# Two transformer blocks on one core: raw tokens turned before their norm, the norm's factor at the projections' reads, and three reorderings

## The chip, the cores and the metric

One NeuronCore of one Trainium2 chip runs the whole program. The time is device microseconds of one execution; three runs of the kernel before took 998.76, 1000.24 and 1002.35 us, median 1000.24. Lower is better.

## What is computed

256 tokens of width 1024, float32, go through two blocks. Cut to what matters here:

```python
def first_block(x, ...):                       # x: (1, 256, 1024)
    h = rms_norm(x, norm_mix)                  # x / sqrt(mean(x^2) + 1e-6) * gain, per token
    q_a, k_a, v_a, q_b, k_b, v_b, g_a, g_b = split(h @ w_in)
    q_a, k_a, q_b, k_b = their own rms_norm per head of 64
    o_a = neighbourhood_attention(q_a, k_a, v_a, rpb)   # 8 heads, a bias gathered from rpb
    o_b = sliding_window_attention(q_b, k_b, v_b, sink, t5_table)
    y = sigmoid(g_a) * (o_a @ w_branch_a) + sigmoid(g_b) * (o_b @ w_branch_b)
    x = x + y @ w_out
    h = rms_norm(x, norm_ffn)
    return x + (silu(h @ w_gate) * (h @ w_up)) @ w_down

def second_block(x, ...):                      # retention + RWKV, then 32 experts of width 512, top 2
    x = x + mixers(rms_norm(x)) @ w_out_2
    x = x + hier_moe(rms_norm(x), ...)         # reads all 32 experts' weights, 192 MB
    return rms_norm(x) * gain
```

rms_norm divides each token by one number, so `rms_norm(x) @ W` equals that number times `(x * gain) @ W`, row by row.

## The kernel before

The program is written out by hand, one instruction list per engine, joined by semaphores. There is no scheduler: each engine's order is the order of the code in its block. A matrix product in float32 precision is made of three passes over rounded parts. Weights and features are each split into a high part (ScalarE copies them rounded, `high_part(g)`, L2183, for weight chunk g; `high_features` and `high_resid` for features) and a low part (VectorE subtracts the high part, `low_part(g)`, L2642; `low` and `resid_low` for features), and TensorE multiplies high by high, high by low and low by high (L1195 to L1197, and L1330 with L1332 in the feed-forward part).

**The front.** SyncE loads the tokens `x` in two halves of 128, then the weights of `w_in`. TensorE first runs 19 idle products (`idle`, L1160). ScalarE squares and sums each half of x (`squares(0)`, L2162) and takes the root (L2163), VectorE inverts it and scales the tokens into `xn` (`norm()`, L2612), TensorE turns `xn` (`norm_T`, L1168), VectorE multiplies by the gain while it reads the turned tokens from PSUM (`moved`, L2651; this waits for `cols`, where the gains lie), ScalarE makes their high parts (L2211), VectorE their low parts (L2657). `moved` and the copies work on quarters (half h of the features, half t of the tokens). `norm_T` also puts the tokens in another order (columns of the 4 x 64 grid in blocks of 8), so that the projected rows come out in that order. Then TensorE runs the projections p1,0 to p1,8 of `w_in`; p1,0 is `first_unit` (L1274), whose first weights ScalarE splits in two steps (`first_high`, L2190). ScalarE copies each projected bank out of PSUM (L2272, L2270 and L2320, plain copies).

**The bias of the first attention.** GpSimd copies `rpb` to DRAM in four DMAs (L1055), waits for weight slot 2 and for the four, and gathers the bias from there with 32 DMAs (L1065) into `biasA_raw`; after them come its copies of the values (`vspan`, `vb`), then 16 loads of the second bias. VectorE adds the window's mask (`biasA_raw` to `biasA`, 8 instructions, L2760). In the code this stands after the heads' norms of p1,0 and p1,1 (`low_part(8)`) and ahead of the sums of squares of p1,3 (L2730, L2734) and of `low_part(9)`, on which the projection p1,5,0 waits. p1,4's sums, the first softmax step `softmax_in(0)` (L2712 to L2721), the norms of q_b and k_b (L2749, L2747) and `low_part(10)` follow.

**The attention loop.** Step i of 9 has on TensorE scores(i), the turning of the probabilities of step i-1 (`turned`), half a projection unit, and the weighted sum of step i-1 (`weighted`, L1471 and L1142). On VectorE it has `softmax_in(i)`, `low_part`, and `weighted(i-1)`, which begins with the copy of the turned probabilities out of PSUM (L2767), on which TensorE's weighted sum waits.

**The residual's turns.** While the output projection `wo` runs, the new x is turned again for the feed-forward part in four pieces j = 0 to 3 of 256 features (`resid_turned`, L1540, and `resid_T` for the last, L1150), each after VectorE has added the piece's projection to x (L2833). VectorE applies the gain (`resid_gain`, L2625), ScalarE makes the high part (`high_resid`, L2196) and VectorE the low part (`resid_low`, L2634). Piece 3 is turned before the first product of the gate; the gate's product takes its features in the order k = 0 to 5 and then 6 to 7. `squares(1)` on ScalarE and `diagonals(1)` on VectorE then make the token factors that `spread_tiles(1)` (L1191) needs inside the first `up` product.

**The experts.** In the last half of the span SyncE streams the experts' weights; each load waits until the place that it fills has been read.

Of the kernel before, what the change touches and what calls it, by code (L numbers as in the profile page):

```python
# [342 lines left out]
def build(nc, A, out):  # L343
# [13 lines left out]
    with ExitStack() as ctx:  # L357
# [73 lines left out]
        bonus = st[:, 160:176]  # L431
        minus_k_a = st[:, 180:184]
# [156 lines left out]
        xn_ready = sem("xn_ready")  # L589
        diag_ready = sem("diag_ready")  # L590
# [73 lines left out]
        rpb_copies = nc.dram_tensor("rpb_copies", (ROWS_A * RUN + 2, 8, ROWS_A * 31), F32, kind="Internal").ap()  # L664
        vb_rows = nc.dram_tensor("vb_rows", (T, P), F32, kind="Internal").ap()
# [245 lines left out]
        def _(sp):  # L911
# [45 lines left out]
            def moe_stream(r, first):  # L957
                if first:
# [40 lines left out]
                    sp.wait_ge(xn_ready, 2 * NT)  # L999
# [51 lines left out]
        def _(pool):  # L1051
# [5 lines left out]
            pool.wait_ge(slot_in[2], 16)  # L1057
# [64 lines left out]
        def _(pe):  # L1122
# [144 lines left out]
            def first_unit(name):  # L1267
# [50 lines left out]
            def features_both(key, name, c, lows=None, between=None):  # L1318
# [74 lines left out]
            idle(19)  # L1393
            pe.wait_ge(ident_in, 16)
            norm_T()

# [155 lines left out]
            resid_T(1, 3, ("wo", 1, 1))  # L1552
# [582 lines left out]
            pe.wait_ge(xn_ready, 2 * NT)  # L2135
# [13 lines left out]
        def _(act):  # L2149
# [88 lines left out]
            high_part(2)  # L2238
# [17 lines left out]
            for n in range(9):  # L2256
# [12 lines left out]
                if u == 4:  # L2269
                    empty(fn(nat[:, :, 2048:2304], bank("p1", 4, 0).rearrange("p (t n) -> p t n", t=NT), ACT.Copy), "p1", 4, 0)  # L2270
                else:
                    empty(fn(nat[:, c, 512 * u:512 * u + 512], bank("p1", u, c), ACT.Copy), "p1", u, c)  # L2272
# [1069 lines left out]
```

## Time and profile before

| | |
|---|---|
| median of three runs | 1000.24 us (998.76 to 1002.35) |
| the profiled execution, its own time | 998.47 us |
| its span | 996.7 us |
| TensorE busy | 867.2 us (87%) |
| VectorE busy | 443.7 us (45%) |
| ScalarE busy | 328.1 us (33%) |
| GpSimd busy | 48.2 us (5%) |
| DMA moved | 293.44 MB, mean 294 GB/s |
| TensorE's granted clock | full in the first 23 of the page's 40 slices, 0.7 to 0.9 and over in the rest |

Busy shares are means over parts with different limits. A TensorE instruction's length in the timeline includes its filling and draining; the distance between two starts is what it costs in a row (0.23 us for 512 columns, 0.12 us for 256).

### The profile page before, as it was taken

What the parts mean: (1) busy time and instruction counts of PE and PEld (TensorE: products, weight loads), DVE (VectorE), ACT (ScalarE), POOL (GpSimd) and SP (SyncE); (2) the same over time, 40 slices, a digit from 0 to 9 for tenths busy, and PEclk for the clock granted to TensorE, in tenths of its full rate; (3) what the DMA queues carried; (4) which work ended last, traced back from release to release, by engine and by line L of the source; (5) the groups of instructions that cost most, each with busy time, mean ns of one, the idle gap of its engine ahead of it and who ended that gap; (6) DMA issues with size and microseconds to landing.
All of it is one profiled execution on the core that took longest, in us unless ns stands there. A gap on an engine that the chain in (4) does not pass through costs nothing.

```text
span 996.7 us, 16047 instructions
## 1 busy us (share of the span) xinstructions
PE 867.2 (87%) x6902; PEld 596.3 (60%) x6902; DVE 443.7 (45%) x593; ACT 328.1 (33%) x433; POOL 48.2 (5%) x80
## 2 busy tenths in 40 slices
PE   9999999899999999999989987667768676785785
PEld 8889888888888889989989532221312221131223
DVE  6766777688776348898865310000100000010002
ACT  6466663665465328645523300000000000000002
POOL 1825000000000000000100000000000000000000
PEclk9999999999999999999999999878978877788889
DMA  9998335486555455452369999999999999999995
GB/s 321 219 339 196 110 114 180 132 283 207 181 171 207 172 177 203 147 192 86 117 203 410 369 429 418 430 428 427 428 429 429 427 428 429 427 430 428 423 424 205
DMA packets 76762, 293.44 MB, mean 294 GB/s; under 512 B 6550, under 2 KB 33430, under 8 KB 63385
## 3 DMA queue, kind: packets, MB, share of 16 engines
q1 hardware_dynamic: 70496, 283.91, 73.4%
q0 software_dynamic: 2592, 3.20, 2.0%
q10 hardware_dynamic: 3608, 5.39, 1.6%
q8 instruction: 49, 0.80, 0.3%
q14 instruction: 17, 0.13, 0.0%
HBM read 288.65 MB, written 3.41 MB: 293 GB/s over the span
## 4 chain that ended last, share of the span: by engine, by line
PE 58%; DMA 31%; DVE 5%; POOL 2%; issue 2%; SPq 1%; ACT 1%; DVEq 0%; ACTq 0%; POOLq 0%
DMA arena<-in_w_up 11%; DMA arena<-in_w_gate 9%; PE psum L1330 8%; DMA arena<-in_w_down 8%; PE psum L2056 7%; PE psum L1195 5%; PE psum L1197 5%; PE psum L1196 5%; PE psum L1357 4%; PE psum L1332 4%; PE psum L2084 3%; PE psum L1731 2%; POOL arena L1065 2%; DVE ring_rounded L2642 1%; DMA arena<-in_w_in 1%
## 5 line engine op out<-in xcount | busy, mean ns | idle before, releaser
L2056 PE MATMUL psum<-arena,featL 128*32 128x512 f32 x1008 | 161.6, 701 | 57.4 <-DMA arena<-in_w_up 38.9
L2642 DVE TENSOR_TENSOR ring_rounded<-arena,hi_rounded 128x2048 fp32r<-128x2048 f32 x75 | 171.6, 2290 | 59.7 <-ACT hi_rounded L2183 58.5
L2183 ACT ACTIVATE hi_rounded<-arena 128x2048 fp32r<-128x2048 f32 x76 | 144.8, 1912 | 85.7 <-DMA arena<-in_w_up 19.8
L2056 PEld LDWEIGHTS psum<-arena,featL 128*32 128x32 f32 x1008 | 37.7, 125 | 168.2 <-issue 85.9
L1330 PE MATMUL psum<-ffn_in_rounded,hi_rounded 128*128 128x512 f32 x352 | 122.3, 394 | 0.0
L2084 PE MATMUL psum<-arena,featT 128*32 128x512 f32 x424 | 76.7, 729 | 38.1 <-DMA arena<-in_w_down 33.8
L1195 PE MATMUL psum<-hi_rounded,featT_rounded 128*128 128x256 f32 (+1 forms) x320 | 101.2, 316 | 1.1 <-DVE ring_rounded L2642 0.9
L1197 PE MATMUL psum<-hi_rounded,featL_rounded 128*128 128x256 f32 (+1 forms) x320 | 99.2, 310 | 0.0
L1196 PE MATMUL psum<-ring_rounded,featT_rounded 128*128 128x256 f32 (+1 forms) x320 | 99.1, 310 | 0.0
L1332 PE MATMUL psum<-ffn_in_rounded,ring_rounded 128*128 128x256 f32 x352 | 97.8, 278 | 0.0
L1330 PEld LDWEIGHTS psum<-ffn_in_rounded,hi_rounded 128*128 128x128 f32 x352 | 66.1, 188 | 15.2
L3228 DVE TENSOR_TENSOR featT<-featT,psum 128x512 f32<-128x512 f32 x8 | 8.2, 1031 | 149.1 <-PE psum L2056 149.1
L2084 PEld LDWEIGHTS psum<-arena,featT 128*32 128x32 f32 x424 | 16.9, 130 | 88.8 <-DMA arena<-in_w_down 46.9
L1332 PEld LDWEIGHTS psum<-ffn_in_rounded,ring_rounded 128*128 128x128 f32 x352 | 66.2, 188 | 0.0
L1195 PEld LDWEIGHTS psum<-hi_rounded,featT_rounded 128*128 128x128 f32 x320 | 61.0, 191 | 4.8 <-ACT arena L2270 1.1
L1197 PEld LDWEIGHTS psum<-hi_rounded,featL_rounded 128*128 128x128 f32 x320 | 61.0, 191 | 3.2
L1196 PEld LDWEIGHTS psum<-ring_rounded,featT_rounded 128*128 128x128 f32 x320 | 61.1, 191 | 3.0
L3213 DVE TENSOR_TENSOR featL<-psum,gain 128x256 f32<-128x256 f32 x32 | 13.6, 425 | 105.3 <-PE psum L2036 105.3
L2545 ACT ACTIVATE featT<-psum 128x512 f32<-128x512 f32 x8 | 4.8, 597 | 163.0 <-PE psum L2056 163.0
L3241 DVE COPY featL<-psum 128x512 f32<-128x512 f32 x7 | 4.8, 692 | 119.2 <-PE psum L2084 119.2
L2547 ACT ACTIVATE featT<-psum 128x512 f32<-128x512 f32 x8 | 4.8, 597 | 132.5 <-PE psum L2072 132.5
L2036 PEld LDWEIGHTS psum<-featT,xn 128*128 128x128 f32 x256 | 32.5, 204 | 17.1 <-issue 14.4
(389 smaller groups left out, 1289.2 us busy)
## 6 DMA issues: line engine op xcount, KB each, us to landing
arena<-in_w_down SPq DMA_DIRECT2D x32, 2048.0 KB, 17.9
arena<-in_w_gate SPq DMA_DIRECT2D x28, 2048.0 KB, 20.7
arena<-in_w_up SPq DMA_DIRECT2D x24, 2048.0 KB, 23.8
arena<-in_w_in SPq DMA_DIRECT2D x14, 2048.0 KB, 9.6
arena<-in_w_up SPq DMA_DIRECT2D x25, 1024.0 KB, 9.1
arena<-in_w_gate SPq DMA_DIRECT2D x14, 1024.0 KB, 5.5
arena<-in_w_down SPq DMA_DIRECT2D x7, 1024.0 KB, 9.8
arena<-in_w_out SPq DMA_DIRECT2D x3, 2048.0 KB, 7.7
```

What stands on the lines that cost most here:

```text
L1065: nc.gpsimd.dma_start(biasA_raw[at % P + RUN * r:at % P + RUN * r + RUN, at // P].rearrange("p h (r c) -> p (h r) c", c=SPAN), src).then_i ...
L1195: mm(o, lhs[0], rhs[0], start=start, stop=False, skip_group_check=True)
L1196: mm(o, lhs[0], rhs[1], start=False, stop=False, skip_group_check=True)
L1197: return mm(o, lhs[1], rhs[0], start=False, stop=stop, skip_group_check=True)
L1330: mm(banks[f].rearrange("p (s t) -> p s t", s=2), hi_cols(g, k, P * f, P), ffn_both[:, :, k, :], start=k == 0, stop=k == DK - 1, skip_grou ...
L1332: ins = mm(banks[f][:, 0:T], lo_cols(g, k, P * f, P), ffn_parts[0][:, k, :], start=False, stop=k == DK - 1, skip_group_check=True)
L1357: return mm(b[:, f, :], w(g, k, P * f, P), r[:, k, :], start=(f, k) == (0, 0) and w is hi_cols and r is featR, stop=stop, skip_group_check ...
L2036: ins = mm(b[:, k - ks[0], :], xn[:, t, k * P:(k + 1) * P], G[:, t].rearrange("p e s -> p (e s)"), start=t == 0, stop=t == NT - 1)
L2056: ins = mm(psum[32 * j:32 * j + 32, MB[4 + m], :], xg[:, 4 * half + k, 32 * j:32 * j + 32], weights(m, half, j, 512 * k), start=half == 0 ...
L2084: return mm(psum[32 * j:32 * j + 32, MB[4 + half], :], hhT[:, k, 32 * j:32 * j + 32], weights(2, k // 2, j, at_), start=k == 0, stop=k == ...
L2183: fn(high, view, ACT.Copy).then_inc(hi_ready, 1)
L2642: tt(low, view, high.bitcast(F32), ALU.subtract).then_inc(lo_ready, 1)
```

## The change

The tokens are turned as they land; the norm's factor is made later and applied as the scale of ScalarE's copies out of PSUM. Since the projected rows stand in the grid's order, GpSimd takes the factors through DRAM into that order (`token_rms`). The number of idle products goes from 19 ahead of the turns to 10 ahead and 6 behind. Four orders change with it: the quarters and first weights at the start, the mask on the bias, the copy of the probabilities, and the residual's turns.

```diff
 @@ GpSimd
-            pool.wait_ge(slot_in[2], 16)
+            pool.wait_ge(rms0_ready, NT)
+            by_place = rms_rows.rearrange("(b r c) a -> r b (c a)", r=ROWS_A, c=RUN)
+            for r in range(ROWS_A):
+                at = GRID_W * (r % 2)
+                nc.gpsimd.dma_start(by_place[r], st[at:at + GRID_W, r // 2:r // 2 + 1], allow_slow_non_contiguous=True)\
+                    .then_inc(rms0_stored, 16)
+            pool.wait_ge(rms0_stored, 16 * ROWS_A)
+            nc.gpsimd.dma_start(token_rms, rms_rows.rearrange("(t p) a -> p (t a)", p=P), allow_slow_non_contiguous=True)\
+                .then_inc(rms0_in, 16)
             pool.wait_ge(rpb_copied, 16 * ROWS_A)
 @@ TensorE
-                        pe.wait_ge(xn_ready, t + 1)
+                        pe.wait_ge(x_in[t], 16)
-                            ins = tr(b[:, k], xn[:, t, (4 * h + k) * P:(4 * h + k + 1) * P], ident)
+                            ins = tr(b[:, k], x[:, t, (4 * h + k) * P:(4 * h + k + 1) * P], ident)
...
+                pe.wait_ge(feat_lo, NT)
+                for t in range(NT):
+                    part(0, t, featLR, hi_cols, range(2))
                 pe.wait_ge(hi_ready, chunk_of[name, 0] + 1)
                 for t in range(NT):
                     part(0, t, featR, hi_cols, range(2, 4))
-                pe.wait_ge(feat_lo, NT)
-                for t in range(NT):
-                    part(0, t, featLR, hi_cols)
+                    part(0, t, featLR, hi_cols, range(2, 4))
...
-                for ks in (range(DK),) if lows is None else (range(0, 6), range(6, DK)):
+                for ks in (range(DK),) if lows is None else (range(0, 4), range(4, 6), range(6, DK)):
                     for f in range(2):
+                        if lows is not None and (ks[0], f) == (0, 1):
+                            resid_turned(turned_bank, 3, ("wo", 1, 1))
...
-            idle(19)
+            idle(10)
             pe.wait_ge(ident_in, 16)
             norm_T()
+            idle(6)
...
-            resid_T(1, 3, ("wo", 1, 1))
+            turned_bank = begin("nt", 1, 3)
 @@ ScalarE
-            squares(0, lambda t: act.wait_ge(x_in[t], 16))
+            fn(warm[:], eps_col[:, 0:1], ACT.Sqrt)
+            high_features((0, 0), (0, 1))
             first_high(0, first_hi)
-            high_features((0, 0), (0, 1))
             first_high(1, hi_ready)
+            high_features((1, 0))
             high_part(1)
-            high_features((1, 0), (1, 1))
+            high_features((1, 1))
+            squares(0, lambda t: act.wait_ge(x_in[t], 16), warmed=True)
+            high_part(2)
...
-                    empty(fn(nat[:, c, 512 * u:512 * u + 512], bank("p1", u, c), ACT.Copy), "p1", u, c)
+                    act.wait_ge(rms0_in, 16)
+                    empty(fn(nat[:, c, 512 * u:512 * u + 512], bank("p1", u, c), ACT.Copy, scale=token_rms[:, c:c + 1]), "p1", u, c)
...
-                    ins = fn(sig[:, :, 256 * i:256 * i + 256], bank("p1", u, c).rearrange("p (t n) -> p t n", t=NT), ACT.Copy)
+                    for t in range(NT):
+                        ins = fn(sig[:, t, 256 * i:256 * i + 256], bank("p1", u, c)[:, 256 * t:256 * t + 256], ACT.Copy,
+                                 scale=token_rms[:, t:t + 1])
...
-            high_resid(1, 0)
+            for j in range(2):
+                high_resid(1, j)
             high_part(first["ffn", 0])
-            high_resid(1, 1)
+            high_resid(1, 2)
             high_part(first["ffn", 0] + 1)
-            for j in range(2, 4):
-                high_resid(1, j)
+            high_resid(1, 3)
 @@ VectorE
-                for t in range(NT):
-                    ts(xn[:, t, :], x[:, t, :], inverse(0, t), None, ALU.mult).then_inc(xn_ready, 1)
...
+                for t in range(NT):
+                    dve.wait_ge(rms_ready, t + 1)
+                    s = st[:, t:t + 1]
+                    nc.vector.reciprocal(s, s).then_inc(rms0_ready, 1)
...
             for u, lo, H in units_:
                 wait_emptied(dve, "p1", u, 0 if u == 4 else 1)
                 q = nat[:, :, lo:lo + 64 * H]
+                if u == 4:
+                    mask_bias()
...
-                if i < 8:
-                    if i:
-                        softmax_in(i)
+                if 0 < i < 8:
+                    softmax_in(i)
+                if i >= 1:
+                    turned(i - 1)
+                if i < 8:
                     low_part(first["p1", 5] + i + 1)
...
-            for c in range(2):
+            projected(0)
+            low_part(first["ffn", 0])
+            resid_gain(1, 2)
+            projected(1)
+            resid_low(1, 2)
+            resid_gain(1, 3)
+            resid_low(1, 3)
             low_part(first["ffn", 0] + 1)
```

`mask_bias` holds the eight additions and their waits as before; `turned` is the copy that began `weighted`; `projected(c)` is the addition to x (L2833 before). The three `xn_ready` counts elsewhere fall by two. p1,4's copy is split in two like the gates'.

The places at which the order matters most:

VectorE around the heads' norms, before. `ring_rounded` rows are `low_part` (the one with hi_rounded_50 is chunk 8, with hi_rounded_59 chunk 9, with hi_rounded_56 chunk 10), `arena<-arena,cst` is the mask, `arena<-psum,arena` the first softmax step.

```order
L2749 TENSOR_TENSOR arena<-arena,st 128x512 x4
L2642 TENSOR_TENSOR ring_rounded<-arena,hi_rounded_50 128x2048
L2760 TENSOR_TENSOR arena<-arena,cst 128x8x32 x8
L2730 TENSOR_TENSOR arena<-arena 128x1024
L2734 TENSOR_REDUCE st<-arena 128x16
L2642 TENSOR_TENSOR ring_rounded<-arena,hi_rounded_59 128x8x256
L2730 TENSOR_TENSOR arena<-arena 128x2x128
L2734 TENSOR_REDUCE st<-arena 128x4
L2712 SCALAR_TENSOR_TENSOR arena<-psum,arena 128x2x128
```

The same place in the changed kernel:

```order
L2786 TENSOR_TENSOR arena<-arena,st 128x512 x4
L2661 TENSOR_TENSOR ring_rounded<-arena,hi_rounded_50 128x2048
L2767 TENSOR_TENSOR arena<-arena 128x1024
L2771 TENSOR_REDUCE st<-arena 128x16
L2661 TENSOR_TENSOR ring_rounded<-arena,hi_rounded_59 128x8x256
L2754 TENSOR_TENSOR arena<-arena,cst 128x8x32 x8
L2767 TENSOR_TENSOR arena<-arena 128x2x128
L2771 TENSOR_REDUCE st<-arena 128x4
L2734 SCALAR_TENSOR_TENSOR arena<-psum,arena 128x2x128
```

The eight additions moved from ahead of p1,3's sums and chunk 9 to right behind them, ahead of p1,4's sums, the first softmax step and chunk 10.

VectorE during the residual's turns, in the changed kernel (`arena<-psum,cols` is `resid_gain`, `ffn_in_rounded` is `resid_low`, `x<-x,psum` the addition to x). The rows of before at this place are, from the third on, resid_low for piece 1, the addition, `low_part`, gain 2, low 2, the addition, gain 3, low 3.

```order
L2644 TENSOR_TENSOR arena<-psum,cols 128x512 x2
L2653 TENSOR_TENSOR ffn_in_rounded<-arena,ffn_in_rounded 128x512 x2
L2864 TENSOR_TENSOR x<-x,psum 128x2x256
L2661 TENSOR_TENSOR ring_rounded<-arena,hi_rounded_60 128x2048
L2644 TENSOR_TENSOR arena<-psum,cols 128x512
L2864 TENSOR_TENSOR x<-x,psum 128x2x256
L2653 TENSOR_TENSOR ffn_in_rounded<-arena,ffn_in_rounded 128x512
L2644 TENSOR_TENSOR arena<-psum,cols 128x512
L2653 TENSOR_TENSOR ffn_in_rounded<-arena,ffn_in_rounded 128x512
L2661 TENSOR_TENSOR ring_rounded<-arena,hi_rounded_58 128x2048
```

The second addition to x now stands ahead of piece 2's low part, no longer behind it.

GpSimd's DMAs, in the changed kernel:

```order
L1060 DMA rpb_copies<-in_rpb 72x1x124
L1060 DMA rpb_copies<-in_rpb 64x1x124 x2
L1060 DMA rpb_copies<-in_rpb 72x1x124
L1066 DMA rms_rows<-st 8x8x1 x4
L1069 DMA st<-rms_rows 128x2x1
L1078 DMA arena<-rpb_copies 8x32x32 x32
L1083 DMA arena<-arena 96x512
```

The five small DMAs of the factor stand ahead of the 32 loads of the bias.

## Rows read from the trace of the kernel before

**Rows 1.** The page: how busy the DMA engines are in 40 equal slices.

```profile
DMA  9998335486555455452369999999999999999995
```

**Rows 2.** TensorE's waits over the span: who for, us in total, times, longest.

```profile
PE psum L2056 <- DMA arena<-in_w_up: 38.9, 15, 4.9
...
PE psum L1195 <- DVE ring_rounded L2642: 0.9, 1, 0.9
PE psum L1142 <- DVE arena L2767: 0.9, 3, 0.3
...
PE psum L1471 <- DVE arena L2767: 0.6, 1, 0.6
```

**Rows 3.** Timeline, start: start us, us, engine, line, what, count [idle before <- releaser].

```profile
1.16 6.88 PE L1160 MATMUL psum<-late 128*128 128x128 f32 x38 [1.16 <-DVE late L2693]
1.20 0.45 ACTq L2226 DMA_DIRECT2D cols<-in_cols  x1
...
6.04 1.06 ACT L2162 ACTIVATE xn<-x 128x1024 f32<-128x1024 f32 x1
...
7.42 1.05 ACT L2190 ACTIVATE hi_rounded<-arena 128x1024 fp32r<-128x1024 f32 x1
...
7.88 2.21 PE L1168 MATMUL psum<-cst,xn 128*128 128x128 f32 x16
...
8.62 1.42 DVE L2651 TENSOR_TENSOR featL<-psum,cols 128x512 f32<-128x512 f32 x2
9.34 1.35 ACT L2211 ACTIVATE featT_rounded<-featL 128x512 fp32r<-128x512 f32 x2 [0.87 <-DVE featL L2651]
...
10.84 2.09 PE L1274 MATMUL psum<-hi_rounded,featT_rounded 128*128 128x512 f32 x8 [0.76 <-ACT featT_rounded L2211]
```

**Rows 4.** DMA issues: transfer, count, KB each, median us from issue to landing.

```profile
cols<-in_cols ACTq DMA_DIRECT2D x1, 35.0 KB, 5.0
...
rpb_copies<-in_rpb POOLq DMA_DIRECT2D x2, 34.9 KB, 5.3
...
rt<-vb_rows POOLq DMA_DIRECT2D x4, 32.0 KB, 2.4
```

**Rows 5.** Timeline of GpSimd's DMA issues.

```profile
17.18 2.44 POOL L1055 DMA_DIRECT2D rpb_copies<-in_rpb  x4 [16.72 <-DMA arena<-in_w_in]
24.88 20.27 POOL L1065 DMA_DIRECT2D arena<-rpb_copies  x31 [5.27 <-DMA rpb_copies<-in_rpb]
52.12 0.66 POOL L1065 DMA_DIRECT2D arena<-rpb_copies  x1 [6.97 <-issue]
```

**Rows 6.** Timeline, 25 to 74 us, TensorE, VectorE and ScalarE.

```profile
25.77 0.58 ACT L2272 ACTIVATE arena<-psum 128x512 f32<-128x512 f32 x1
...
32.74 0.39 PE L1195 MATMUL psum<-hi_rounded,featT_rounded 128*128 128x512 f32 x1
...
57.10 2.77 DVE L2760 TENSOR_TENSOR arena<-arena,cst 128x256 f32<-128x256 f32 x8 [7.21 <-DMA arena<-rpb_copies]
...
59.98 1.92 ACT L2183 ACTIVATE hi_rounded<-arena 128x2048 fp32r<-128x2048 f32 x1
...
62.42 2.29 DVE L2642 TENSOR_TENSOR ring_rounded<-arena,hi_rounded 128x2048 fp32r<-128x2048 f32 x1
...
69.57 2.29 DVE L2642 TENSOR_TENSOR ring_rounded<-arena,hi_rounded 128x2048 fp32r<-128x2048 f32 x1
...
73.09 0.36 PE L1195 MATMUL psum<-hi_rounded,featT_rounded 128*128 128x256 f32 x1
```

**Rows 7.** Timeline, 180 to 194 us, TensorE and ScalarE.

```profile
180.68 0.66 PE L1540 MATMUL psum<-cst,x 128*128 128x128 f32 x4 [1.03 <-DVE x L2833]
...
185.76 0.63 PE L1150 MATMUL psum<-cst,x 128*128 128x128 f32 x4 [1.54 <-DVE x L2833]
...
187.22 0.64 ACT L2196 ACTIVATE ffn_in_rounded<-arena 128x512 fp32r<-128x512 f32 x1 [3.00 <-DVE arena L2625]
...
193.16 0.61 PE L1191 MATMUL psum<-rt,cst 128*128 128x128 f32 x4
```

More of the change, by code:

```diff
@@ L431, in build @@
         bonus = st[:, 160:176]
+        token_rms = st[:, 10:10 + NT]
         minus_k_a = st[:, 180:184]
@@ L589, in build @@
         xn_ready = sem("xn_ready")
+        rms0_ready = sem("rms0_ready")
+        rms0_stored = sem("rms0_stored")
+        rms0_in = sem("rms0_in")
         diag_ready = sem("diag_ready")
@@ L2269, in _ @@
                 if u == 4:
-                    empty(fn(nat[:, :, 2048:2304], bank("p1", 4, 0).rearrange("p (t n) -> p t n", t=NT), ACT.Copy), "p1", 4, 0)
-                else:
-                    empty(fn(nat[:, c, 512 * u:512 * u + 512], bank("p1", u, c), ACT.Copy), "p1", u, c)
+                    for t in range(NT):
+                        ins = fn(nat[:, t, 2048:2304], bank("p1", 4, 0)[:, 256 * t:256 * t + 256], ACT.Copy, scale=token_rms[:, t:t + 1])
+                    empty(ins, "p1", 4, 0)
+                else:
+                    act.wait_ge(rms0_in, 16)
+                    empty(fn(nat[:, c, 512 * u:512 * u + 512], bank("p1", u, c), ACT.Copy, scale=token_rms[:, c:c + 1]), "p1", u, c)
                 if n == 7:
@@ L2670, in norm_T @@
                 low(0, 1)
+                moved(1, 0)
                 first_low(0, first_hi, first_lo)
                 first_low(1, hi_ready, lo_ready)
-                moved(1, 0)
                 moved(1, 1)
@@ L2677, in norm_T @@
                 low_part(1)
+                for t in range(NT):
+                    dve.wait_ge(rms_ready, t + 1)
+                    s = st[:, t:t + 1]
+                    nc.vector.reciprocal(s, s).then_inc(rms0_ready, 1)
             def low_moved(*key):
@@ L2721, in softmax_in, with mask_bias @@
                     ts(m, m, -1.0, None, ALU.mult).then_inc(max_ready, 1)
+            def mask_bias():
+                dve.wait_ge(params_in, PARAMS_IN)
+                dve.wait_ge(biasA_in, 16 * 8 * ROWS_A)
+                for t in range(NT):
+                    for b in range(SPAN // RUN):
+                        raw = biasA_raw[:, t].rearrange("p h (r c) -> p h r c", r=ROWS_A)[:, :, :, RUN * b:RUN * b + RUN]
+                        made = biasA[:, t].rearrange("p h (b r c) -> p h b r c", r=ROWS_A, c=RUN)[:, :, b]
+                        window = con("wina")[:, SPAN * t + RUN * b:SPAN * t + RUN * b + RUN]
+                        ins = tt(made, raw, window.unsqueeze(1).unsqueeze(1).to_broadcast([P, 8, ROWS_A, RUN]), ALU.add)
+                ins.then_inc(biasA_ready, 1)
+                dve.wait_ge(biasA_ready, 1)
             tmp = area(L1, "probT", 4, 512)[:, 0:2, :]
@@ L2751, in _, with turned @@
                     low_part(8)
-                    dve.wait_ge(params_in, PARAMS_IN)
-                    dve.wait_ge(biasA_in, 16 * 8 * ROWS_A)
-                    for t in range(NT):
-                        for b in range(SPAN // RUN):
-                            raw = biasA_raw[:, t].rearrange("p h (r c) -> p h r c", r=ROWS_A)[:, :, :, RUN * b:RUN * b + RUN]
-                            made = biasA[:, t].rearrange("p h (b r c) -> p h b r c", r=ROWS_A, c=RUN)[:, :, b]
-                            window = con("wina")[:, SPAN * t + RUN * b:SPAN * t + RUN * b + RUN]
-                            ins = tt(made, raw, window.unsqueeze(1).unsqueeze(1).to_broadcast([P, 8, ROWS_A, RUN]), ALU.add)
-                    ins.then_inc(biasA_ready, 1)
-                    dve.wait_ge(biasA_ready, 1)
+            def turned(i):
+                wait_filled(dve, "PT", i, 1)
+                kn = NT if i >= 4 else 1
+                empty(nc.vector.tensor_copy(probT[:, 2 * (i % 2) + 1, :, 0:kn, :],
+                                            bank("PT", i, 1).rearrange("p (a k q) -> p a k q", a=2, k=2)[:, :, 0:kn, :]), "PT", i, 1)
             def weighted(i):
                 br, t, g = i // 4, i // 2 % 2, i % 2
-                wait_filled(dve, "PT", i, 1)
-                kn = NT if br else 1
-                empty(nc.vector.tensor_copy(probT[:, 2 * (i % 2) + 1, :, 0:kn, :],
-                                            bank("PT", i, 1).rearrange("p (a k q) -> p a k q", a=2, k=2)[:, :, 0:kn, :]), "PT", i, 1)
                 if i == 7:
@@ L2829, in _, with projected @@
                 resid_low(1, j)
-            for c in range(2):
+            def projected(c):
                 wait_filled(dve, "wo", 1, c)
@@ L2833, in _ @@
                 empty(tt(xs, xs, bank("wo", 1, c).rearrange("p (t n) -> p t n", t=NT), ALU.add), "wo", 1, c)
-                if c == 0:
-                    low_part(first["ffn", 0])
-                resid_gain(1, 2 + c)
-                resid_low(1, 2 + c)
+            projected(0)
[5 more added lines that the diff above has]
+            resid_low(1, 3)
             low_part(first["ffn", 0] + 1)
```

8 lines of the change are left out of this document (3 added, 5 removed).

## The prediction

> **What bounds the kernel now.** I read the page's slices first, then TensorE's waits, then the timeline of three places. The slices show two parts: from slice 5 to 21 the DMA engines are at 2 to 8 tenths, from slice 22 on at 9 tenths or more without a break [rows 1]. In the waits TensorE's long ones are all for experts' weights, the longest group 38.9 us for w_up [rows 2]; so the second part is a DMA stream. It cannot be made shorter by this change, but its loads are released by TensorE's and VectorE's progress through the first part, so whatever the first part gains moves the whole stream and the end by the same amount. I take that carry as one to one. In the first part TensorE hardly ever waits, so an edit is worth only what it takes from or adds to TensorE's few gaps: the start before p1,0 (10.84 us [rows 3]), 0.9 us for the low part of chunk 9, 0.6 and 0.9 us for the copy of the probabilities [rows 2], and 1.03 and 1.54 us for the additions to x [rows 7].
>
> **1. The start.** TensorE begins p1,0 at 10.84 [rows 3]. With the tokens turned raw, the chain is: the second half of x is there by 6.04; the gains `cols`, needed for the first read of the turned tokens, are issued at 1.20 and land 5.0 later, at 6.2 [rows 3, 4]. Before, they were no limit; now they are the first one. Two gains of 0.71 (1.42 for two) end at 7.7, the copy of the second quarter (0.68, half of 1.35) at 8.4, the first weights' high part (1.05; they were there by 7.42) at 9.5. TensorE's own list: 12 turns after 6.04, at 0.11 to 0.14 each (16 took 2.21 with a break in them), end at 7.4 to 7.7, six idle products at 0.36 (19 took 6.88) end at 9.6 to 9.9 [rows 3]. So p1,0 starts at about 9.7: **1.1 us earlier** (ends 0.9 and 1.3). Behind it each split is ready before its matmul: by the same durations the second chunk's high features stand at 14.1 and are wanted at 9.7 + 24 x 0.23 = 15.2, its low weights at 17.1 and are wanted at 9.7 + 40 x 0.23 = 18.9. The squares moved behind them on ScalarE run while weights land. What VectorE loses of work there (two scalings) is no term.
>
> **2. The factor's way.** New on GpSimd: four stores and one load. GpSimd is free of the four rpb copies at 19.6 (17.18 + 2.44) [rows 5] and the factors are inverted at about 17.4, behind `low_part(1)`. At 0.61 per issue the last store is issued at 21.4. No row of before shows a DMA this small under load; the nearest are the rpb copies, 5.3 us to landing while weights stream, and the vb loads, 2.4 with the stream thin [rows 4]. Both legs at 2.4 give 26.4, both at 5.3 give 32.2; the stream is dense until p1,3's weights are in, so I take the first leg at 5.3 and the second between: back at about 30.6. ScalarE's copy of the first p1 bank was at 25.77 [rows 6] and now waits for this, and everything behind it on ScalarE too: the high part of chunk 5, then the other banks, p1,3's chunks, the root. The first of them that TensorE wants is chunk 5, at the middle of p1,2: 32.74 - 1.1 + 24 x 0.23 = 37.2. Back from there go 0.15 and 2.29 for the low part, 1.92 for the high part, 0.6 for the copy [rows 6]: the factor may come by 32.2. At 30.6 it costs **nothing**, cover 1.6 us; beyond 32.2 each microsecond costs one.
>
> The Trainium skill (DMA: Bandwidth & Descriptors, Anatomy of one DMA, SWDGE path) gives a DMA issued by GpSimd a fixed cost of about 2.0 us. By that the factor would be back near 26 and the second rival below would have no chance. The 5.3 us of the row disagrees with it under load, and I go by the row.
>
> **3. The mask on the bias.** Before, it held VectorE until 57.10 and was 2.8 us long; chunk 9's low part followed at 62.42, 0.5 after its high part (59.98 + 1.92), and TensorE waited 0.9 for it [rows 2, 6]. Now p1,3's sums go ahead of the bias's arrival, and the low part starts with the high part's end, at 61.95 less the 1.1 of the start: 60.8, so 1.6 earlier than before. But the mask now stands between it and p1,4's sums, the first softmax step, the norms of q_b and k_b and chunk 10's low part. That low part began at 69.57 and ended at 71.86; TensorE wanted it at 73.09, a slack of 1.1 after 0.15 of passing on [rows 6]. Now: 71.86 - 1.6 + 2.8 + 0.15 = 73.2. So p1,5,1 starts at 73.2 instead of 73.09: the start's gain and the 0.9 us wait are both spent here, **0.1 us lost** net. In between TensorE waits for the norms of q_b and k_b instead. The general form is: start's gain less 1.2.
> This holds while the bias is there. Its last load landed at 57.1, 32.2 us after the first was issued at 24.88, with a stall of 6.97 before the 32nd [rows 5, 6]. With the factor's DMAs ahead it starts near 27.4, and by the same 32.2 us is in at 59.6. The mask wants it at 63.1 (60.8 + 2.3): cover 3.5 us.
>
> **4. The copy of the probabilities.** It goes ahead of a `low_part` of 2.29 [rows 6], on which TensorE waits a unit later. The waits on L2767, 0.6 + 0.9 [rows 2], should go: **1.5 us**. VectorE then has the low part 0.4 to 0.7 later; it was ready some 2 us ahead of its product. After this TensorE alone sets the loop.
>
> **5. The split copies.** One 128x512 copy becomes two of half the length, with their own start; some 0.15 us each more on ScalarE, which has gaps in every step of the loop: **nothing**. If the loop became ScalarE's, eight times 0.15 would cost 1.2.
>
> **6. The residual's turns.** Both waits on the addition (1.03 and 1.54) go [rows 7]. The first, since ScalarE no longer puts weights ahead of piece 1's high part and VectorE comes to the addition when the product ends; the second, since piece 3 is turned inside the gate's product, after its first four features. What is late next: the squares, which need ScalarE behind piece 3's high part. In before the spread at 193.16 came 5.94 after that high part began at 187.22 [rows 7]. Now the high part begins at about 185.5 (TensorE reaches the gate at 182.9, runs four features, 1.4, turns, 0.4, gain 0.7), so the spread may come by 191.4, or earlier if the 5.94 held slack; that is a gain of 1.7 to 2.6 in place of 2.57. I take **2.1 us**.
>
> **Sum.** -0.1 + 1.5 + 2.1 = 3.5 us faster. Against the profiled execution, 998.47 - 3.5 = 995.0. That execution lies 1.8 under the median of 1000.24; from the median it is **996.7 us**. A measurement of this kernel tells about 0.3%, 3.0 us, from no change, so the forecast lies just beyond.
>
> **Rivals.**
> *The late factor.* Both legs take more than 5.3 us and the factor comes at 34.4 instead of before 32.2. For: small DMAs under a dense stream, the five stand in a row, each leg waits for all of the one before. Against: the stream pauses after p1,3's load. Then ScalarE is late, TensorE waits 2.2 in p1,2, and since chunk 9 hangs on TensorE's turns this goes through: 996.7 + 2.2 = 998.9.
> *The residual gains half.* ScalarE's high parts collide with the squares, or the low part of the `up` weights, now ahead of nothing, is late: 1.0 instead of 2.1, and 997.8. For: VectorE's list is full between 176 and 191. Against: each step has a place worked out above.
> *Slower: the bias comes late.* The five small DMAs stand ahead of the 32 loads, and the stall of 6.97 shows that GpSimd's queue can stop for a reason no row gives. If it stops once more, for another 7 to 10 us, the bias is in at 66.6 to 69.6 or beyond, VectorE stands at the mask with the first softmax step, the norms and chunk 10 behind it, and TensorE waits one for one past 63.1. It cancels the gain from 66.6 and is slower by over 0.3% from 69.6. For a bias at 70.1: 996.7 + 7.0 = 1003.7. For: everything now hangs on GpSimd's one list, and the factor has to come first. Against: 3.5 us of cover, and the bytes added are nothing.
> *It does less than it says at the start:* p1,0 gains under 0.9, because idle products and `cols` hold it. Each tenth lost there is a tenth of the end; it lies in the range.
>
> **How the numbers follow.** The forecast with its small errors has 0.62, the late factor 0.16, the half residual 0.16, the late bias 0.06. Within the forecast's own case 995.0 to 997.9, some 0.5 of its 0.62 lie beyond 3.0 us, and some 0.05 come from the others when a favourable median meets them: faster 0.55. Same 0.39, slower 0.06. The range goes from the best bounds (start 1.3, residual 2.6, 4.2 together, and about 2 for how medians of three scatter) at 994.1 to the late factor and its scatter at 999.5.
>
> **What would show it.** In the changed profile: TensorE's first product near 9.7; ScalarE's first scaled copy near 30.6, waiting for the DMA of the factor, and no wait of TensorE in p1,2; the mask at about 63.1, not waiting for a DMA, and TensorE waiting for norms and chunk 10 around 69 to 73, with p1,5,1 starting at 73.2; no wait for the probabilities' copy; no wait for the addition to x, and the spread 3.5 us earlier than 193.16. It is wrong if p1,5,1 starts earlier than 72.5 or later than 74, if the spread's gain over that point is under 3 us, or if the experts' stream does not carry it to the end.

## The result and the profile after

| | before | after |
|---|---|---|
| median | 999.58 us (998.76 to 1002.35, 4 runs) | 1008.43 us (1007.11 to 1012.79, 4 runs) |
| the profiled execution, its own time | 998.47 us | 1007.11 us |
| its span | 996.7 us | 1005.3 us |

The ratio is 1.0093 (95% interval 1.0068 to 1.0119): the change costs about 9 us. The forecast was 996.7 us, 3.5 faster, with a range up to 999.5.

The page of after. The DMA engines' second slice (25 to 50 us) no longer holds the rate of before [rows 1], and TensorE's granted clock dips in the same slice:

```profile
PEclk9799999999999999999999998788977878787889
DMA  9789535575665436454349999999999999999995
```

TensorE's waits between 8 and 200 us (what, for whom, us in total, times, longest):

```profile
PE psum L1208 <- DVE ring_rounded L2661: 9.7, 3, 8.6
PE psum L1163 <- DVE arena L2786: 0.6, 1, 0.6
PE psum L1287 <- ACT hi_rounded L2207: 0.5, 1, 0.5
PE psum L1208 <- DVE featL_rounded L2711: 0.3, 1, 0.3
PE psum L1346 <- DVE ring_rounded L2661: 0.3, 1, 0.3
```

Of before's waits [rows 2, 7], those for the probabilities' copy and for the additions to x are gone, as forecast. One is new: 8.6 us for the low part of a weight chunk. The timelines of GpSimd's issues, of ScalarE and of TensorE show where it comes from:

```profile
19.82 2.24 POOL L1066 DMA_DIRECT2D rms_rows<-st  x4
34.74 0.74 POOL L1069 DMA_DIRECT2D st<-rms_rows  x1 [12.68 <-DMA rms_rows<-st]
35.47 20.27 POOL L1078 DMA_DIRECT2D arena<-rpb_copies  x31
63.46 0.66 POOL L1078 DMA_DIRECT2D arena<-rpb_copies  x1 [7.71 <-issue]
```

```profile
40.79 0.69 ACT L2294 ACTIVATE arena<-psum,st 128x512 f32<-128x512 f32 x1 [12.11 <-DMA st<-rms_rows]
41.51 1.91 ACT L2200 ACTIVATE hi_rounded<-arena 128x2048 fp32r<-128x2048 f32 x1
```

```profile
9.64 1.20 PE L1287 MATMUL psum<-hi_rounded,featT_rounded 128*128 128x512 f32 x4 [0.47 <-ACT hi_rounded L2207]
...
45.79 0.79 PE L1208 MATMUL psum<-hi_rounded,featT_rounded 128*128 128x512 f32 x1 [8.65 <-DVE ring_rounded L2661]
...
200.59 0.68 PE L1204 MATMUL psum<-rt,cst 128*128 128x128 f32 x4 [0.21 <-DVE rt L2635]
```

The start is earlier by 1.2. GpSimd issued the four stores of the factor by 22.06, waited 12.68 for them, and the load was back at 40.7. ScalarE stood 12.11 for it; behind it on its list was the high part of the chunk that TensorE needs in the middle of p1,2, and TensorE stood 8.65. The last line is the spread (`spread_tiles(1)`), the mark at which the first part's gain or loss is read: 200.59, against 193.16 before [rows 7].

The stores took more than their own time. Here are stretches of 2 us of after. Each row gives the busy us of PE, PEld, DVE, ACT and POOL, then TensorE's granted clock, the DMA share and GB/s. Then the same stretches of before:

```profile
24.00:26.00 2.00, 2.00 (x10) 1.65 (x10) 0.00 (x0) 0.00 (x0) 0.00 (x0) 1.00 1.20 133
26.00:28.00 2.00, 2.00 (x11) 1.65 (x10) 0.00 (x0) 1.24 (x1) 0.00 (x0) 1.00 1.17 189
28.00:30.00 2.00, 2.00 (x11) 1.65 (x10) 1.29 (x1) 0.68 (x1) 0.00 (x0) 1.00 1.50 105
...
40.00:42.00 2.00, 0.00 (x0) 0.00 (x0) 0.00 (x0) 1.18 (x2) 2.00 (x4) 0.50 0.43 55
...
46.00:48.00 2.00, 2.00 (x5) 1.61 (x6) 1.97 (x3) 1.97 (x2) 2.00 (x4) 0.50 0.41 51
```

```profile
24.00:26.00 2.00, 2.00 (x11) 1.65 (x10) 0.10 (x1) 2.00 (x2) 1.12 (x2) 1.00 0.94 334
26.00:28.00 2.00, 2.00 (x11) 1.65 (x10) 2.00 (x1) 1.97 (x2) 2.00 (x4) 1.00 1.04 407
28.00:30.00 2.00, 2.00 (x10) 1.68 (x9) 1.86 (x2) 0.78 (x2) 2.00 (x4) 1.00 1.12 312
```

While 1 KB of factors goes out, the rate is 105 to 189 GB/s where before it was 312 to 407, and the DMA engines count as no less busy. TensorE stopped at about 37; from 39.4 on it is granted 0.50 (1.2 GHz), and still when it works again (5 products between 46 and 48).

### The profile page after: what moved, and what is told of

It reads as the page before. It is cut to its first block, busy times and chain, and to the rows that moved or that the text cites. A ratio compares the mean times of both kernels' runs of the same rounds, so it can differ in the third digit from the quotient of the medians.

```text
span 1005.3 us, 16049 instructions
## 1 busy us (share of the span) xinstructions
PE 872.4 (87%) x6896; PEld 598.3 (60%) x6896; DVE 442.3 (44%) x591; ACT 331.0 (33%) x442; POOL 51.2 (5%) x85
## 4 chain that ended last, share of the span: by engine, by line
PE 61%; DMA 31%; DVE 3%; ACT 1%; SPq 1%; issue 1%; POOL 0%; DVEq 0%; ACTq 0%
DMA arena<-in_w_up 11%; DMA arena<-in_w_gate 9%; DMA arena<-in_w_down 8%; PE psum L1346 8%; PE psum L2073 7%; PE psum L1208 6%; PE psum L1210 6%; PE psum L1209 6%; PE psum L1373 4%; PE psum L1348 4%; PE psum L2101 3%; PE psum L1748 2%; DMA arena<-in_w_in 1%; DMA rms_rows<-st 1%; PE psum L1245 1%; PE psum L1244 1%
## 5 line engine op out<-in xcount | busy, mean ns | idle before, releaser
L1346 PE MATMUL psum<-ffn_in_rounded,hi_rounded 128*128 128x512 f32 x352 | 124.8, 399 | 0.3 <-DVE ring_rounded L2661 0.3
## 6 DMA issues: line engine op xcount, KB each, us to landing
arena<-in_w_in SPq DMA_DIRECT2D x14, 2048.0 KB, 10.9
```

The costliest lines, as they stand in the source:

```text
L1346: mm(banks[f].rearrange("p (s t) -> p s t", s=2), hi_cols(g, k, P * f, P), ffn_both[:, :, k, :], start=k == 0, stop=k == DK - 1, skip_grou ...
```

## The experiments

Three theories stood against each other. **Theory 1:** the four stores, 256 separate 4-byte elements, hold up all DMA queues, their own included; the late factor is the whole loss, and all other terms are right. **Theory 2:** only the trip through GpSimd's queue under a dense stream is slow, whatever is stored; the weights' low rate has another reason. **Theory 3:** the loss lies in the new orders of start or mask. Each kernel was timed against the kernel before on the same chip; its medians there were 999.13 us (experiments 1, 2, 3 and 9), 1000.08 (4, 5, 6 and the first of 10), 998.95 (512 bytes apart, the first of 8, the second of 10), 999.55 (64 bytes apart) and 999.19 (the rest).

**1. Without the trip.** The factors' way into the grid's order is left out.

```diff
-token_rms = st[:, 10:10 + NT]
+token_rms = st[:, 0:NT]
-pool.wait_ge(rms0_ready, NT)
...
+pool.wait_ge(slot_in[2], 16)
-act.wait_ge(rms0_in, 16)
+act.wait_ge(rms0_ready, NT)
```

> The changed kernel without the factor's way through memory: ScalarE reads the inverted factors where VectorE leaves them, so the factors stand at the wrong tokens; four stores and a load are left out, all else is the change. Theory 1 (the four stores of single 4-byte elements hold up all DMA queues, and the late factor is the whole loss): no wait of 8.6 us in p1,2, weights of p1,3 land near 31, the bias near 57, p1,5,1 starts at 73.2, the spread at 189.6, and the kernel is 3.5 us faster than before: about 996. Theory 2 (only the factor is late, the weight stream was slow for another reason): the wait goes too, but the rate stays low between 24 and 32 us; 996 to 998. Rival (the loss lies in the new order of the mask or of the start): 1003 or more.

996.0 us, ratio 0.9968 (0.9955 to 0.9982), and 366 instead of 133 GB/s from 24 to 26. Its timeline of TensorE, and its line for the spread:

```profile
69.73 1.23 PE L1154 MATMUL psum<-cst,arena 128*128 128x128 f32 x8 [0.56 <-DVE arena L2777]
73.21 0.36 PE L1199 MATMUL psum<-hi_rounded,featT_rounded 128*128 128x256 f32 x1 [0.61 <-DVE ring_rounded L2652]
...
189.79 0.68 PE L1195 MATMUL psum<-rt,cst 128*128 128x128 f32 x4 [0.21 <-DVE rt L2626]
```

p1,5,1 starts at 73.21 (the forecast's 73.2) and the spread comes at 189.79, 3.4 ahead of before [rows 7]. Theory 3 falls; the whole loss is in the trip, and without it the kernel is 3 us faster than before.

**2. The orders alone**, on the kernel before: `turned(i - 1)` ahead of `low_part`, and the residual's new order.

> The kernel before with only the probability copies moved ahead of the low part and the residual's turns reordered. By the sum of the prediction 1.5 + 2.1 = 3.6 us faster than before: about 996, spread at 189.5 instead of 193.2. If the gain after the spread is given back later in the program (the changed kernel ended 1.2 us later than its spread would give), 997 to 998.

997.21 us, ratio 0.9989 (0.9972 to 1.0006); the spread at 189.94, 3.2 earlier. In this profile p1,0 began 0.5 later than in before's (11.30 against 10.84), with nothing changed there. From p1,5,1 (73.25) to the spread it is 116.7 against 120.1, so terms 4 and 6 give 3.4 where 3.6 was forecast; less of it is in the time, for which see below.

**3. The trip alone**, on the kernel before, nobody reading its result.

```diff
+pool.wait_ge(xn_ready, NT)
+for r in range(ROWS_A):
+    at = GRID_W * (r % 2)
+    nc.gpsimd.dma_start(by_place[r], st[at:at + GRID_W, r // 2:r // 2 + 1], allow_slow_non_contiguous=True)\
+        .then_inc(rms0_stored, 16)
+pool.wait_ge(rms0_stored, 16 * ROWS_A)
+nc.gpsimd.dma_start(token_rms, rms_rows.rearrange("(t p) a -> p (t a)", p=P), allow_slow_non_contiguous=True)\
+    .then_inc(rms0_in, 16)
-pool.wait_ge(slot_in[2], 16)
```

> The kernel before with the four stores and the load added on GpSimd at the same place, and nobody who waits for the factor. Theory 1 (the stores themselves hold up the other queues): between 22 and 32 us the rate falls to about half or less, weight packets get several times longer, the stores take about 12 us to land and the weights of p1,3 land near 37; bias loads start near 35 and the bias comes 9 us later (66), so VectorE waits at its mask and the kernel is 5 to 9 us slower. Theory 2 (the change of the stream comes from something else in the changed kernel): the rate between 22 and 32 stays as before, the stores land in about 5 us each, and the bias comes 4 to 6 us later.

1010.03 us, ratio 1.0109 (1.009 to 1.0128), with nobody waiting for the factor. GpSimd's list, and a stretch of its windows:

```profile
31.69 0.75 POOL L1068 DMA_DIRECT2D st<-rms_rows  x1 [9.60 <-DMA rms_rows<-st]
```

```profile
24.00:26.00 2.00, 2.00 (x11) 1.65 (x10) 0.00 (x0) 0.00 (x0) 0.00 (x0) 1.00 0.35 41
26.00:28.00 2.00, 2.00 (x10) 1.67 (x9) 0.00 (x0) 0.00 (x0) 0.00 (x0) 1.00 0.60 51
28.00:30.00 2.00, 2.00 (x10) 1.67 (x9) 0.00 (x0) 0.00 (x0) 0.00 (x0) 1.00 0.87 35
```

41, 51 and 35 GB/s against before's 334, 407 and 312. The five DMAs do this by themselves. TensorE waits 9.6 in four pieces: three of 1.6, 1.4 and 1.2, and the longest (5.4) behind VectorE's mask, which stands in its old place and now waits for the bias. From 74 to 80 TensorE is granted 0.50 of its clock.

**4. Two of the four stores, unread, and no load.**

> The kernel before with two of the four stores added, no load, nobody who reads them; GpSimd waits for their landing before it issues the bias loads. If each 4-byte element costs the engines its share, the stall is about half as long as with four (9.6 us of waiting becomes about 5, TensorE's waits for weights 9.6 become 2 to 5) and the kernel is 3 to 6 us slower than before; with four it was 10.9. If the stall doesn't depend on the number (a fixed cost of the first one), as with four.

1005.63 us, ratio 1.0063 (1.0042 to 1.0085): 5.6 slower, where four stores and the load cost 10.9. GpSimd's wait, and the first and last of these stretches:

```profile
28.00 20.30 POOL L1075 DMA_DIRECT2D arena<-rpb_copies  x31 [7.05 <-DMA rms_rows<-st]
```

```profile
24.00:26.00 2.00, 2.00 (x11) 1.65 (x10) 0.00 (x0) 0.00 (x0) 0.00 (x0) 1.00 0.46 54
...
28.00:30.00 2.00, 2.00 (x10) 1.66 (x9) 0.92 (x1) 1.97 (x3) 2.00 (x4) 1.00 0.99 367
```

With four stores (experiment 3) it was low for two stretches more, of which this is the second:

```profile
30.00:32.00 2.00, 2.00 (x10) 1.65 (x10) 0.00 (x0) 1.60 (x1) 0.31 (x1) 1.00 0.56 17
```

So the low rate lasted from 24 to 28 with two stores and from 24 to 32 with four: it grows with the number of elements. GpSimd's wait does so less clearly (7.05 against 9.60, where about 5 was expected), and the time says little on it, since the weights' delay itself cost nothing here: TensorE's one new wait, 7.1, is for the bias again.

**5. The stores from ScalarE's queue.**

> The changed kernel with the four 4-byte-element stores issued by ScalarE on its hardware queue, the load still on GpSimd. If the 4-byte writes themselves stall the DMA engines: the rate between 22 and 32 falls all the same, the factor is back after 38 and the time is 1003 to 1010. If GpSimd's software queue is the cause: stores down in 3 to 5 us, rate undisturbed, 996 to 999.

1005.67 us, ratio 1.0043 (1.0026 to 1.006):

```profile
24.00:26.00 2.00, 2.00 (x11) 1.65 (x10) 0.00 (x0) 0.00 (x0) 0.00 (x0) 1.00 1.24 72
```

```profile
32.18 0.75 POOL L1063 DMA_DIRECT2D st<-rms_rows  x1 [12.55 <-DMA rms_rows<-st]
```

Issued 1.5 us earlier, the stores hold the rate down all the same (61 to 92 GB/s up to 34), and the scaled copy starts at 38.86. It is not GpSimd's queue that makes the stores slow.

**6. The factor widened to a row of 512 bytes**, stored by the same four DMAs.

```diff
-nc.vector.reciprocal(s, s).then_inc(rms0_ready, 1)
+link(nc.vector.reciprocal(s, s))
+ts(xn[:, t, 0:P], late[:, 0:P], s, None, ALU.mult).then_inc(rms0_ready, 1)
-nc.gpsimd.dma_start(by_place[r], st[at:at + GRID_W, r // 2:r // 2 + 1])
+nc.gpsimd.dma_start(by_place[r], xn[at:at + GRID_W, r // 2, 0:P])
```

> The changed kernel with each factor widened by VectorE to a row of 128 equal numbers (512 bytes) before the four stores; the load takes one of each row, still 4 bytes each. If the 4-byte writes are what holds up the queues: stores down within about 5 us, weights land near 31 as in the kernel without the trip, the factor is back between 30 and 33, TensorE waits under 1 us in p1,2, and the time is 996 to 999. If it is the round trip in GpSimd's queue under a dense stream, whatever the size: as the changed kernel, 1006 or more.

997.76 us, ratio 0.9978 (0.9963 to 0.9993). The DMA issues (KB each, median us to landing):

```profile
rms_rows<-xn POOLq DMA_DIRECT2D x4, 32.0 KB, 5.2
```

```profile
24.00:26.00 2.00, 2.00 (x11) 1.65 (x10) 0.00 (x0) 1.42 (x1) 0.00 (x0) 1.00 1.00 320
```

128 times the bytes land sooner (the stores of after took 7.3 by their median). Theory 2 falls; but this changes two things, the size of an element and where it lies, and the next four part them.

**7. The same 4-byte elements, spaced in memory** (only the row length of `rms_rows` and the column used differ): 512 bytes apart, 64 apart, 64 apart at byte 4 of each 64, and 32 apart.

```diff
-rms_rows = nc.dram_tensor("rms_rows", (T, 1), F32, kind="Internal").ap()
+rms_rows = nc.dram_tensor("rms_rows", (T, P), F32, kind="Internal").ap()
-by_place = rms_rows.rearrange("(b r c) a -> r b (c a)", r=ROWS_A, c=RUN)
+by_place = rms_rows[:, 0:1].rearrange("(b r c) a -> r b c a", r=ROWS_A, c=RUN)
```

> The changed kernel with the same 4-byte elements stored 512 bytes apart in memory instead of side by side; the load reads them there. If what costs is that many engines write into the same few bytes of memory (1 KB in all): the stores are down in about 5 us, the rate between 24 and 34 recovers and the time is 996 to 999. If each 4-byte write costs for its size wherever it goes: as the changed kernel, stores 10 us or more, time 1006 to 1010.

> The changed kernel with the 4-byte elements stored 64 bytes apart (512 apart cured it; side by side cost 12 us; whole rows of 64 bytes side by side cost nothing). If writes disturb each other only within the same 64 bytes: stores down in about 5 us, factor back near 30, rate undisturbed, 995 to 998.5. If a partly written neighbourhood larger than 64 bytes is what costs: stores 8 us or more and 1000 to 1010.

> As the kernel with 4-byte elements 64 bytes apart, but each at byte 4 of its 64 bytes instead of byte 0. If elements disturb each other only by sharing 64 bytes: as that kernel, stores down in about 5 us, 995 to 998.5. If what costs is a write that starts off a 32- or 64-byte boundary, as 7 of 8 did in the changed kernel: stores 10 us or more, 1004 to 1010.

> The 4-byte elements 32 bytes apart, so two in each 64 bytes, each at a 32-byte boundary. If sharing 64 bytes is what costs: between the two, stores 6 to 9 us, 998 to 1004. If sharing 32 bytes or an unaligned start is: as 64 apart, about 5 us, 995 to 998.5.

Medians 997.5, 997.1, 996.19 and 995.91 us; ratios 0.9992 (0.9977 to 1.0006), 0.998 (0.9959 to 1.0001), 0.9977 (0.9961 to 0.9994) and 0.9976 (0.9961 to 0.9992). The DMA issues with 512 apart, then with 32 apart:

```profile
rms_rows<-st POOLq DMA_DIRECT2D x4, 0.2 KB, 5.0
...
st<-rms_rows POOLq DMA_DIRECT2D x1, 1.0 KB, 2.4
```

```profile
rms_rows<-st POOLq DMA_DIRECT2D x4, 0.2 KB, 5.5
...
st<-rms_rows POOLq DMA_DIRECT2D x1, 1.0 KB, 2.2
```

and the stretch from 26 to 28 us with 512 apart, 389 GB/s:

```profile
26.00:28.00 2.00, 2.00 (x10) 1.68 (x9) 2.00 (x1) 0.00 (x0) 0.77 (x2) 1.00 1.05 389
```

The size of the element costs nothing. Nor does a start off a boundary (byte 4 is as good as byte 0). What costs is that the elements lie 4 bytes apart: spacing them by eight words cures it whole. So theory 1 holds in a narrower form: not small writes, but small writes side by side. 8 and 16 bytes apart weren't tried. Nor was it parted whether an element is disturbed by its nearest neighbours or by all that go into the same small stretch of memory (1 KB side by side, 8 KB at 32 bytes apart); what happens in the memory no run shows.

**8. Rows of 64 bytes side by side**, the widening of experiment 6 with 16 columns, timed twice.

> The changed kernel with each factor stored as a row of 16 equal numbers, 64 bytes, rows side by side. With rows of 512 bytes the stores landed after 5.2 us and nothing was held up. If the cost is one of writes smaller than a memory word of some size at or under 64 bytes: as with 512 bytes, 996 to 999. If 64 bytes are still too few: 1000 to 1010, in between or as the changed kernel.

> The kernel with rows of 64 bytes once more, since it was the fastest of all (ratio 0.9967 to before, 0.9951 to 0.9983) and the others of its kind, which differ from it in the store's layout alone, gave 0.9978, 0.9980 and 0.9992. If all four have the same time: 0.997 to 0.999. If rows of 64 bytes are really better: 0.9955 to 0.9975.

995.4 and 997.27 us; ratios 0.9967 (0.9951 to 0.9983) and 0.9981 (0.9965 to 0.9996). Both intervals lie below 1: it beats the kernel before, by 2 to 3 us, but isn't better than its relatives.

**9. The factors turned on TensorE**, no DMA: two turns of the factor's columns to a row, VectorE's copy in the new order, two products with one column each; p1,1's middle hides the way.

> The changed kernel with the same factors brought to token order on the chip: two turns of the factor columns to a row on TensorE, a copy of the row in the new order by VectorE, two products with one column each, and a copy of two columns; no DMA. All theories in which the trip is the loss: factors there near 27 us, so no wait in p1,2, TensorE pays about 1 us for four small instructions at most, and the time is 995.5 to 997.5. If the loss is elsewhere: 1003 or more.

997.89 us, ratio 0.9985 (0.997 to 0.9999); no wait in p1,2. TensorE pays for it:

```profile
26.19 0.60 PE L1261 MATMUL psum<-late,xn 1*128 1x1 f32 x4
```

With the two turns before it the spread is at 190.58, 0.8 later than in experiment 1.

**10. The same with the mask in VectorE's gap**, `mask_bias()` ahead of `low_part(9)`; timed twice.

> The kernel of the factors turned on TensorE, with the mask put between p1,3's sums and chunk 9's low part: there VectorE stood 4.06 us for chunk 9's high part (57.5 to 61.56) and the bias had landed by 56. If the prediction's term 3 is right (the mask behind chunk 9 costs what the start gains), the waits of 0.6 for the norms and 0.6 for chunk 10 go and the spread comes 1.1 us earlier than in that kernel, near 189.3: 1 us faster than it, about 996.5 by its median, 2.6 faster than before. Rival (the mask costs nothing where it stands, or its new place delays chunk 9): no difference.

> The same kernel as the factors turned on TensorE with the mask in VectorE's gap, timed a second time, since its first interval (0.9969 to 1.0002) leaves open whether it beats the kernel before. Its spread came 3.9 us earlier than before's. If the experts' part carries that on average: a ratio of 0.996 to 0.998. If the pause of TensorE for its own instructions near 520 us (3.2 in the first profile, 0.6 in before's) comes in most of its executions and seldom in before's: 0.9985 or more again, and the profile shows the pause again. If it comes and goes from execution to execution, this profile may be without it.

998.85 and 996.96 us; ratios 0.9985 (0.9969 to 1.0002) and 0.9981 (0.9966 to 0.9995). VectorE's timeline of the first, the mask and chunk 9's low part:

```profile
58.01 2.77 DVE L2761 TENSOR_TENSOR arena<-arena,cst 128x256 f32<-128x256 f32 x8
62.04 2.29 DVE L2662 TENSOR_TENSOR ring_rounded<-arena,hi_rounded 128x2048 fp32r<-128x2048 f32 x1 [1.25 <-ACT hi_rounded L2201]
```

The two waits of 0.6 are gone and the spread came at 189.29 and 188.82, 1.3 and 1.8 earlier than in experiment 9, where 1.1 was expected (counted from the start of p1,0, which was at 9.87, 9.41 and 9.39, p1,5,1 gains 1.8 both times). Term 3 had the place right, and its price was if anything too low. The times can't tell 1 us.

## Why the prediction failed, by its own steps

**Term 1, the start:** forecast 9.7, measured 9.64. Right.

**Term 2, the factor's way: the step that failed.** The order of events behind the factor was right, and so was the rule "beyond 32.2 each microsecond costs one": the factor came 8.5 after 32.2 (40.7) and TensorE stood 8.65. What was wrong is the first leg, taken as 5.3 from the rpb copies [rows 4]; it took 12.7 behind the last issue. The second leg, taken between 2.4 and 5.3, took 6.0. The rows that bounded it all move long pieces of memory; this was 1 KB in 256 adjacent elements of 4 bytes, and the bound had no room for that. "The bytes added are nothing", used against the slower rival, was the very thought that hid it. (By the prediction's own terms the bounds for the factor's return are 26.2 and 32.0, not 26.4 and 32.2, which changes nothing.) With the elements apart the sum came out as forecast: the scaled copy waited until 30.32 with 64 bytes between them (forecast 30.6). The first leg took 5.8 there and the second about 2.5.

```profile
30.32 0.69 ACT L2294 ACTIVATE arena<-psum,st 128x512 f32<-128x512 f32 x1 [3.89 <-DMA st<-rms_rows]
```

The Trainium skill (DMA: Bandwidth & Descriptors, Anatomy of one DMA) has a fixed cost of about 2.0 us for a DMA from GpSimd; under the weight stream they took more in every run: 4.2 to 5.5 for a store and 2.1 to 3.1 for the load where the elements lay apart or were widened. The rival that this weighs on is the late factor, the first of the prediction's list and not the second. Another page of the Trainium skill (Collectives: The Full Stack, Rules for kernel authors) asks for buffers of collectives aligned to 32 bytes, to avoid a read-modify-write in the hardware. It speaks of alignment and not of distance. That elements 32 bytes apart cost nothing is compatible with it; alignment alone is not what counts here, since elements at byte 4 of each 64 cost nothing either.

**Term 3, the mask:** right, but for its size (experiment 10). In after the bias loads began at 35.47 instead of 27.4, yet everything else was late too, and the mask didn't wait for them. Without the trip p1,5,1 starts at 73.21 (73.2).

**Terms 4 to 6:** right. After's waits show it above; from p1,5,1 to the spread the kernel without the trip takes 116.6, before 120.1 [rows 6, 7]: 3.5 gained where 3.6 was forecast.

**The rivals:** the late factor had the right place and the right path to TensorE, and a bound of 34.4, drawn from the same wrong row, so 998.9 and a chance of 0.16. Its reason, small DMAs under a dense stream that wait for one another, was not the cause: experiments 6 and 7 have five DMAs in the same chain under the same stream, and the factor is back by 30.8 in each. The late bias did not hold up the mask in after; it did in experiments 3 and 4, where the mask stands in its old place.

**From trace to time in after:** the product at 45.79 starts 9.03 after the one ahead of it, where 0.23 is usual, so the wait costs 8.8. The nine starts behind it take 3.93 (45.79 to 49.72) instead of 2.04, so 1.9 more are lost at half clock. Together that is 10.7 of the 10.8 by which p1,5,1 starts later than without the trip (84.01 against 73.21). Of the 10.9 by which it is later than before's, 3.5 are gained back behind it, and the spread is 7.4 late. From the spread to the end after takes 804.7 and before 803.5. These 1.2 lie within the scatter of the eight profiles that have no pause of the kind told of next (801.3 to 804.7).

**The carry, "one to one":** right only in part. Seven timings of the change with its stores apart or widened average 0.9979, 2.1 us, where their spreads came 2.7 to 3.6 earlier than before's. Some of it goes into a pause of TensorE near 520 us, in which it waits for nothing that the profile shows. Before, the kernel without the trip, and one with 64 bytes between elements:

```profile
521.13 0.39 PE L1812 MATMUL psum<-xn,arena 64*64 64x64 f32 x6 [0.58 <-issue]
```

```profile
519.88 1.21 PE L1837 MATMUL psum<-arena,featL 128*64 128x64 f32 x13 [2.83 <-issue]
```

```profile
519.41 1.56 PE L1846 MATMUL psum<-arena,featL 128*64 128x64 f32 x13 [2.29 <-issue]
```

The kernel with rows of 64 bytes had no such pause in its first profile (span 991.8) and one of 2.1 in its second (995.7), so it comes and goes with the execution. Whether an earlier first part makes it likelier stays open: before, after and experiments 3 and 4 showed 0.9 at most, while nine of the thirteen other profiles showed 2.1 to 3.4, one of them (2.6) experiment 5's, whose spread was 5.2 later than before's.

The pause costs more than its length. In seven of the nine the granted clock falls to 0.50 in it or up to 1.6 us behind it, and in no other profile near there. Here are four us, first of before and then of the kernel without the trip:

```profile
520.00:524.00 4.00, 3.42 (x68) 3.15 (x65) 2.73 (x7) 1.40 (x5) 0.00 (x0) 1.00 0.90 304
```

```profile
520.00:524.00 4.00, 4.00 (x38) 3.88 (x39) 0.87 (x3) 0.77 (x2) 0.00 (x0) 0.57 1.01 375
```

From the spread to the end the nine profiles take 805.3 to 808.8 (mean 807.1), the other eight 801.3 to 804.7 (mean 802.8). That is enough to hide a gain of 3.5. What TensorE waits for can be read from the traces, though no experiment tested it: in all nine a packet of 16 KB of the DMA queue that the page calls "instruction" starts 2.2 to 2.4 before the pause ends. So it most likely waits for its own program, and why the packet comes late stays open.

## What to carry to other kernels

When a step writes small elements to memory, look first at how near to each other they land: 256 elements of 4 bytes side by side made this kernel 9 us slower where it would have been 2 faster, and slowed the weights of another queue, and the same elements 32 bytes apart cost nothing. A DMA is not priced by its bytes or by a row of another shape; where no row of the same shape exists, the upper bound is open, and the chance belongs there. Work that one list brings for another engine (here ScalarE's first copy) should stand behind what doesn't need it, so that a late transfer holds up only its own readers.

## What the runs showed of the hardware

- 4-byte writes side by side took the rate, most of it the weights of another queue, from 312 to 407 GB/s to 35 to 189 between 24 and 30 us, from either issuing queue. With two stores the low rate lasted 4 us, with four 8. 32, 64 and 512 bytes apart it stayed at 276 to 396 up to 28.
- GpSimd's stall of 6.97 ahead of the 32nd bias load [rows 5] came in all 17 profiles at the same load, 7.0 to 8.5 long, with no, one, two or five more DMAs of GpSimd ahead of it. So it isn't a count of its DMAs; its cause stays open.
- TensorE's clock fell to 0.50 (1.2 GHz) during the wait of 8.65 and came back at about 49.6, 3.8 us after work had begun. It also fell in the waits of 5.4, 7.1 and 4.3 of experiments 3, 4 and 5.
- TensorE paused 2.1 to 3.4 us near 520 us in nine of 17 profiles, for nothing that it lists as awaited. A packet of the instruction queue stood 2.2 to 2.4 ahead of each pause's end, and in seven the clock fell to 0.50 with it.
